# Second mixers of a hybrid model on one core: memory sums one step later, memory tiles one a beat, attention output turned behind two half products

## The chip, the core and the metric

The kernel runs on one core of one Trainium2 chip. The metric is the device time of the whole program in microseconds (us). The core has five engines that work through their own queues of instructions and wait for each other by semaphores: PE (TensorE, matrix products), ACT (ScalarE), DVE (VectorE), POOL (GpSimd) and SP (SyncE, which here issues the loads of the weights). PEld is PE's loading of the stationary operand, which overlaps its products.

## What is computed

A hybrid model of three layers on 512 tokens of width 1024, all in float32. The first layer and the final normalisation are not touched here. Two further layers follow, each: feed-forward, hybrid mixer, attention over a memory of 256 tokens, feed-forward.

```python
def second_block(x, mem, ...):
    for l in range(DEPTH_2):                      # 2
        y = swiglu_2(rms_norm(x, ffn1_pre_g[l]), ...)
        x = x + 0.5 * rms_norm(y, ffn1_post_g[l])
        y = hybrid_mixer(rms_norm(x, mix_pre_g[l]), w_in[l], ..., nsa_out_g[l], ret_gn_g[l], w_out[l])
        x = x + rms_norm(y, mix_post_g[l])
        y = memory_xattn(rms_norm(x, xa_pre_g[l]), rms_norm(mem, xa_mem_g[l]),
                         xa_wq[l], xa_wk[l], xa_wv[l], xa_wo[l])
        x = x + rms_norm(y, xa_post_g[l])
        y = swiglu_2(rms_norm(x, ffn2_pre_g[l]), ...)
        x = x + 0.5 * rms_norm(y, ffn2_post_g[l])
    return x

def hybrid_mixer(h, w_in, cmp_pe, cmp_w1, cmp_w2, nsa_out_g, ret_gn_g, w_out):
    parts = jnp.split(h @ w_in, IN_OFFSETS, axis=-1)
    ...
    o_nsa = rms_norm(nsa_mixer(...), nsa_out_g)    # attention: 8 heads, 3 branches
    o_ret = retention(...)                         # 4 heads, 4 chunks
    return jnp.concatenate([o_nsa, o_ret], axis=-1) @ w_out
```

`memory_xattn` needs the keys `rms_norm(mem) @ wk` and the values `rms_norm(mem) @ wv`. They don't depend on the tokens, and the kernel makes them inside the hybrid mixer.

## The kernel before

**Products.** Every float32 product is made of three: each operand is split into a high part (rounded to PE's fast format) and a low part (the rest), and `mm3` adds hi·hi, hi·lo and lo·hi in one PSUM bank (lines 251 to 253). Weights come in chunks of 1024 x 256, each as two halves of 128 x 1024. For each half SP loads `raw`, ACT copies it to `whi` (`weight_hi`, L234), and POOL subtracts `whi` from `raw` to give `wlo` (`weight_lo`, L246). There are four slots, so a chunk is split while the chunk two before it is in use: `weight_hi(k, ch.c + 2)` waits until that chunk has released its slot.

**The order.** Each engine's program is written out by hand as Python generators. A `yield` ends a *beat*. In `MixerTwo` the attention of 96 units (4 blocks of queries x 8 heads x 3 branches) sets the frame: in each step PE makes the scores of unit s (L933), turns the weights of unit s-1 (L944) and multiplies unit s-2 with the values (L957); DVE adds the bias and takes the maximum (L1000, L1004); ACT takes the exponent (L972) and copies the turned weights (L981). After each step come two beats of *filler*: products of the projections (`pe_filler`), 196 beats in all. Four streams run beside the filler: after every fourth beat one step of the memory's sums (from beat 8), of the retention (from beat 98), and of the norms of finished blocks of queries (from 60, 109, 157). All engines count the same beats; what one engine does in a beat and another needs in the same beat is thus close in time.

**The memory's root mean square.** `act_memory` squares one of eight tiles of the memory in each of its steps (L2219, 128 x 256, two buffers). `pe_memory` sums that square over the features in the same step with four small products (L342). In the step after the last square DVE takes the mean (L2336) and POOL the power -0.5 (L2373, `m_root`); one step further on PE spreads it over the rows (L2129) and ACT keeps the row (L2223). POOL's filler has a `weight_lo` of two halves every 16 beats, among them one at beat 48.

**The memory's tiles.** After the last gate chunk of the retention the filler makes the memory's high and low parts: ACT `xa_mhi` (L2205), DVE `xa_mlo` (L2321), two tiles in each of four beats in which PE has no filler. Then come four chunks of keys (`mkch`, all in banks 6 and 7) and four of values (`mvch`).

**The end of the mixer.** When the attention is done, the last block of queries is normalised: ACT square and sum (L2186), DVE mean (L2302), POOL power (L2357), DVE scaling (L2306). Then four times four blocks of it are turned by PE (`TurnTiles.pe`, L1506), and ACT and DVE make the high and low parts (L1514, L1521), which are the operands of w_out. w_out is done in four pairs of banks; the first two chunks, c0 and c1, are done by halves (`pe_out_half`): half 0 uses the retention's output, which is there earlier, half 1 the attention's.

## Time and profile before

| | us |
|---|---|
| median of 3 runs | 3539.95 |
| lowest and highest | 3537.64 and 3546.28 |
| the profiled execution, whole | 3543.9 |
| its span (first to last instruction) | 3542.6 |
| PE busy in the span | 3379.3 |
| ACT, DVE, POOL busy | 1225.6, 1373.4, 1275.5 |
| granted clock of PE, mean | 0.974 of full speed |

The profile lists one execution. Its own time is 3543.9 us, of which 1.3 us lie outside the span. Times in the trace are from the span's start. The first of the two mixers lies at about 1185 to 1635 us, the second at about 2550 to 3000 us; they do the same work in the same order. PE's clock has two levels in the records: 1.00 is 2.4 GHz, 0.50 is 1.2 GHz.

### The profile page before, as it was taken

Reading aid. Unit: us, or ns where it says so; the run is one execution under the profiler, and the core shown is the slowest. Engines: PE = TensorE matmul, PEld = TensorE weight load, DVE = VectorE, ACT = ScalarE, POOL = GpSimd, SP = SyncE. Lnnn points to the kernel's source line nnn. Section 1 sums busy time; section 2 is a strip of 40 time slices with the busy share of each in tenths; the row PEclk is TensorE's granted clock in tenths of the full one; section 3 lists DMA queues with packets and bytes.
Section 4 is the critical chain, followed back from the end, with each engine's and each line's share of the span. In section 5 each row is a group of like instructions: output and inputs, shape, how many; then the busy total and the mean of one; then the engine's idle time right before and its main releaser. Section 6 shows DMA issues by size and latency. Waiting matters only on the chain.

```text
span 3542.6 us, 42038 instructions
## 1 busy us (share of the span) xinstructions
PE 3379.3 (95%) x16296; PEld 2725.8 (77%) x16296; DVE 1373.4 (39%) x2531; ACT 1225.6 (35%) x2245; POOL 1275.5 (36%) x569
## 2 busy tenths in 40 slices
PE   5989999999999999999999999999989999999997
PEld 4876788887888767787678887888776877678886
DVE  4574443215330524654353304331334562534311
ACT  4444332223222433453332223222333444433221
POOL 3332244443444432132234443444351233224442
PEclk9999999999999989999999999999999999999999
DMA  3211122332333221121123222322231112112321
GB/s 126 79 55 53 51 92 96 97 99 79 98 101 98 89 90 44 42 72 66 58 80 99 98 98 75 107 95 94 79 125 48 37 61 83 60 60 95 99 98 66
DMA packets 79109, 287.05 MB, mean 81 GB/s; under 512 B 8896, under 2 KB 9152, under 8 KB 78400
## 3 DMA queue, kind: packets, MB, share of 16 engines
q1 hardware_dynamic: 77616, 278.42, 24.0%
q10 hardware_dynamic: 1296, 5.94, 0.4%
q8 instruction: 131, 2.15, 0.3%
q14 instruction: 66, 0.54, 0.0%
HBM read 282.23 MB, written 2.10 MB: 80 GB/s over the span
## 4 chain that ended last, share of the span: by engine, by line
PE 83%; DVE 7%; ACT 4%; POOL 3%; issue 3%; DMA 0%; ACTq 0%; POOLq 0%; DVEq 0%
PE bank L251 23%; PE bank L252 23%; PE bank L253 23%; PE bank L933 4%; PE bank L957 3%; POOL wlo L246 2%; PE bank L944 2%; ACT whi L234 1%; DVE hlo L620 1%; ACT hhi L668 1%; DVE x L615 1%; PE bank L2632 1%; DVE m_xbc L1542 1%; DVE m_V L2290 1%; PE bank L551 1%
## 5 line engine op out<-in xcount | busy, mean ns | idle before, releaser
L246 POOL TENSOR_TENSOR wlo<-raw,whi 128x1024 fp32r<-128x1024 f32 (+1 forms) x520 | 1230.6, 2367 | 2047.6 <-ACT whi L234 2012.7
L251 PE MATMUL bank<-hhi,whi 128*128 128x512 f32 x2416 | 971.1, 402 | 21.7 <-POOL wlo L246 10.2
L252 PE MATMUL bank<-hlo,whi 128*128 128x512 f32 x2456 | 963.8, 392 | 0.0
L253 PE MATMUL bank<-hhi,wlo 128*128 128x512 f32 x2416 | 949.2, 393 | 0.0
L234 ACT ACTIVATE whi<-raw 128x1024 fp32r<-128x1024 f32 (+1 forms) x536 | 533.7, 1034 | 377.0 <-PE bank L253 361.4
L251 PEld LDWEIGHTS bank<-hhi,whi 128*128 128x128 f32 x2416 | 458.6, 190 | 129.1 <-issue 33.0
L252 PEld LDWEIGHTS bank<-hlo,whi 128*128 128x128 f32 x2456 | 466.5, 190 | 91.6 <-issue 1.5
L253 PEld LDWEIGHTS bank<-hhi,wlo 128*128 128x128 f32 x2416 | 458.0, 190 | 98.0
L251 PE MATMUL bank<-ff_ahi,whi 128*128 128x512 f32 x880 | 342.8, 390 | 0.0
L253 PE MATMUL bank<-ff_ahi,wlo 128*128 128x512 f32 x880 | 342.4, 389 | 0.0
L252 PE MATMUL bank<-ff_alo,whi 128*128 128x512 f32 x840 | 326.8, 389 | 0.0
L493 DVE TENSOR_TENSOR tmp<-tmp,tmp 128x512 f32<-128x512 f32 x60 | 47.7, 795 | 577.4 <-ACT tmp L507 577.4
L972 ACT ACTIVATE att_s<-att_s,stat 128x128 f32<-128x128 f32 (+4 forms) x224 | 110.6, 494 | 426.9 <-DVE stat L1004 426.7
L846 ACT ACTIVATE ff_ahi<-tmp 128x512 fp32r<-128x512 f32 x110 | 69.6, 633 | 444.7 <-DVE tmp L869 444.7
L859 DVE TENSOR_TENSOR tmp<-bank,row 128x512 f32<-128x512 f32 x110 | 75.1, 690 | 365.0 <-PE bank L253 318.9
L253 PEld LDWEIGHTS bank<-ff_ahi,wlo 128*128 128x128 f32 x880 | 165.2, 188 | 34.6
L251 PEld LDWEIGHTS bank<-ff_ahi,whi 128*128 128x128 f32 x880 | 165.2, 188 | 34.0
L252 PEld LDWEIGHTS bank<-ff_alo,whi 128*128 128x128 f32 x840 | 157.7, 188 | 32.5
L1000 DVE SCALAR_TENSOR_TENSOR att_s<-consts,bank 128x32 f32<-128x32 f32 (+4 forms) x192 | 74.2, 386 | 273.6 <-PE bank L933 273.2
L840 ACT ACTIVATE tmp<-tmp 128x512 f32<-128x512 f32 x110 | 68.6, 630 | 308.4 <-DVE tmp L859 308.4
L867 DVE TENSOR_TENSOR tmp<-bank,row 128x512 f32<-128x512 f32 x110 | 75.9, 690 | 223.6 <-PE bank L253 223.6
L251 PE MATMUL bank<-whi,hhi 128*128 128x256 f32 x448 | 134.3, 300 | 0.0
(346 smaller groups left out, 4381.0 us busy)
## 6 DMA issues: line engine op xcount, KB each, us to landing
raw<-wstream SPq DMA_DIRECT2D x516, 512.0 KB, 3.7
raw<-wstream SPq DMA_DIRECT2D x20, 256.0 KB, 3.0
x<-xT ACTq DMA_DIRECT2D x4, 512.0 KB, 12.9
xa_v<-memT ACTq DMA_DIRECT2D x2, 1024.0 KB, 4.8
outT<-x SPq DMA_DIRECT2D x1, 2048.0 KB, 6.2
consts<-consts ACTq DMA_DIRECT2D x1, 1103.0 KB, 9.5
m_lw<-lru_w ACTq DMA_DIRECT2D x1, 544.0 KB, 3.4
par<-par SPq DMA_DIRECT2D x2, 248.0 KB, 13.9
```

Of the source, the lines that this page charges most:

```text
L234: a.activation(h.hi[:, 0:h.cols], h.raw[:, 0:h.cols], ACT.Copy).then_inc(h.hi_made.sem)
L246: g.tensor_tensor(h.lo[:, 0:h.cols], h.raw[:, 0:h.cols], h.hi[:, 0:h.cols].bitcast(F32), ALU.subtract).then_inc(h.lo_made.sem)
L251: t.matmul(out, l[0], r[0], start=start, stop=False)
L252: t.matmul(out, l[0], r[1], start=False, stop=False)
L253: return t.matmul(out, l[1], r[0], start=False, stop=stop)
L859: v.tensor_tensor(k.tmp[m][:, :], k.bank[gate.banks[m]][:, :], k.row[:, :], ALU.mult).then_inc(self.normed.sem)
L867: v.tensor_tensor(k.tmp[m][:, :], k.bank[up.banks[m]][:, :], k.row[:, :], ALU.mult).then_inc(self.up.sem)
L933: t.matmul(k.bank[b][:, 0:u["n"]], u["q"], u["k"], start=True, stop=True).then_inc(self.scores.sem)
L944: last = t.transpose(k.bank[b][0:rows, kb * P:(kb + 1) * P], s[:, kb * P:kb * P + rows], k.c("ident"))
L957: last = t.matmul(k.bank[b][:, at:at + DH], p[0:rows, kb * P:(kb + 1) * P], u["v"](kb), start=kb == 0, stop=kb == nb - 1, skip_group_check ...
L972: a.activation(s[:, 0:n], s[:, 0:n], ACT.Exp, bias=k.stat[:, 80 + step % 4:81 + step % 4], accum_out=self.sums(g)[0][:, step % group:step ...
L1000: v.scalar_tensor_tensor(s[:, 0:n], u["dist"], u["slope"], k.bank[b][:, 0:n], ALU.mult, ALU.add).then_inc(self.biased.sem)
```

## The change

It is made in `MixerTwo` alone (and one flag in a helper), so each part of it runs twice.

1. PE's sums of the squares run one memory step (four beats) behind ACT's squares. The mean on DVE, the power on POOL, the spreading on PE and the row on ACT come one to three steps later than before (DVE one, POOL and PE two, ACT three). DVE waits for the row just ahead of the first keys.
2. The memory's high and low parts are made one tile a beat in eight beats on ACT and DVE. PE starts the first key chunk after three empty beats instead of four, and takes it tile by tile (`pe_first_keys`: both banks for each tile) instead of bank by bank. DVE evicts both banks of that chunk in one beat.
3. At the end PE does half 0 of c0 and of c1 and then turns the attention's output, into four banks (0, 1, 4, 5) instead of two. The split of c1's weights moves on ACT and POOL from ahead of the last norm to behind it.

```diff
@@ MixerTwo.__init__
-        self.cat_nsa.takes(0, 1, 0, 1)
+        self.cat_nsa.takes(0, 1, 4, 5)
@@ MixerTwo.pe
         self.pe_out_half(c0, 0)
+        self.pe_out_half(c1, 0)
         run(self.cat_nsa.pe())
-        self.pe_out_half(c1, 0)
         self.pe_out_half(c0, 1)
         self.pe_out_half(c1, 1)
@@ pe_filler
-        yield from beats(4)
+        yield from beats(3)
         m = [self.mhi, self.mlo]
-        for c, ch in enumerate(self.mkch):
-            yield from pe_stationary(k, ch, lambda n: [a[:, n * MEM:(n + 1) * MEM] for a in m], KT, width=MEM,
-                                     ready=(lambda n: [self.m_lo[n]]) if c == 0 else None)
+        tile = lambda n: [a[:, n * MEM:(n + 1) * MEM] for a in m]
+        yield from self.pe_first_keys(self.mkch[0], tile)
+        for ch in self.mkch[1:]:
+            yield from pe_stationary(k, ch, tile, KT, width=MEM)
...
+    def pe_first_keys(self, ch, tile):
+        k, t = self.k, self.k.nc.tensor
+        for kk in range(KT):
+            pe_half_begin(k, ch, kk)
+            t.wait_ge(*self.m_lo[kk])
+            for m, b in enumerate(ch.banks):
+                if kk == 0 and ch.free[m] is not None:
+                    t.wait_ge(*ch.free[m])
+                last = mm3(k, k.bank[b][:, 0:MEM], ch.weights(kk, m * P, P), tile(kk), kk == 0, kk == KT - 1)
+                pe_step_end(ch, last, kk, kk == KT - 1, m == 1)
+            yield
@@ pe_memory
+        yield
         for n in range(KT):
             t.wait_ge(*self.m_sq[n])
...
-        yield
+        yield from beats(2)
         t.wait_ge(*self.m_root[0])
@@ act
         run(self.act_norm(3))
+        weight_hi(k, self.mvch[3].c + 2)
         weight_hi(k, self.out.chunks[0][4].c + 2, 0)
@@ act_filler
-            if n % 2:
-                yield
-        for c, ch in enumerate(self.mkch):
+            yield
+        yield from idle_act(k, self.mkch[0], 3)
+        for ch in self.mkch[1:]:
             yield from idle_act(k, ch, 8)
...
-            yield from keep_tokens_act(..., self.mv_kept, root=self.m_rs)
+            yield from keep_tokens_act(..., self.mv_kept, root=self.m_rs, then=c < 3)
@@ act_memory
-        yield
+        yield from beats(4)
         a.wait_ge(*self.m_rows[0])
@@ dve_filler
+        yield
         for n in range(KT):
...
-            if n % 2:
-                yield
+            yield
+        yield from beats(2)
+        v.wait_ge(*self.m_row[0])
         for c, ch in enumerate(self.mkch):
             for m, b in enumerate(ch.banks):
-                yield from beats(KT // 2)
+                yield from beats(KT // 2 if c > 0 else 0)
@@ dve_memory
-        yield from beats(KT)
+        yield from beats(KT + 1)
@@ pool
         run(self.pool_norm(3))
+        weight_lo(k, self.mvch[3].c + 2)
         self.out.pool()
@@ pool_filler
-        yield from beats(4)
-        for ch in self.mkch + self.mvch:
+        yield from beats(3)
+        for ch in self.mkch + self.mvch[0:3]:
             yield from idle_pool(k, ch, 8)
+        yield from beats(8)
@@ pool_memory
-        yield from beats(KT)
+        yield from beats(KT + 2)
         g.wait_ge(*self.m_mean[0])
```

**Place 1: POOL at beat 48 of the first of the two mixers.** `stat` is where the memory's mean and its root stand; `raw`, `whi`, `wlo` are the slots of the weights. The queue before:

```order
L246 TENSOR_TENSOR wlo2_61<-raw2_53,whi2_57 128x1024 [waits s_wlo,s_whi]
L246 TENSOR_TENSOR wlo3_62<-raw3_54,whi3_58 128x1024 [waits s_wlo,s_whi]
L2373 TENSOR_TENSOR stat_73<-stat_73,consts_71 128x2 [waits s_rstd_mean]
L246 TENSOR_TENSOR wlo0_59<-raw0_51,whi0_55 128x1024 [waits s_wlo,s_whi]
L246 TENSOR_TENSOR wlo1_60<-raw1_52,whi1_56 128x1024 [waits s_wlo,s_whi]
```

And now:

```order
L246 TENSOR_TENSOR wlo2_61<-raw2_53,whi2_57 128x1024 [waits s_wlo,s_whi]
L246 TENSOR_TENSOR wlo3_62<-raw3_54,whi3_58 128x1024 [waits s_wlo,s_whi]
L246 TENSOR_TENSOR wlo0_59<-raw0_51,whi0_55 128x1024 [waits s_wlo,s_whi]
L246 TENSOR_TENSOR wlo1_60<-raw1_52,whi1_56 128x1024 [waits s_wlo,s_whi]
L2393 TENSOR_TENSOR stat_73<-stat_73,consts_71 128x2 [waits s_rstd_mean]
```

The power for the memory's root has moved behind the two halves of a chunk's low part.

**Place 2: DVE where the memory's low parts begin, first mixer.** `m_gr` is the last gate of the retention, `att_s` and the maximum in `stat` belong to the next unit of the attention, `xa_mlo` is the memory's low part, `tmp_68` the retention's decayed scores. The queue before:

```order
L1084 SCALAR_TENSOR_TENSOR m_gr_121<-tmp_66,bank 128x256 [waits s_silu_tanh]
L2321 SCALAR_TENSOR_TENSOR xa_mlo_155<-xa_v_130,par_49,xa_mhi_154 128x256 [waits s_mem_hi] x4
L1000 SCALAR_TENSOR_TENSOR att_s_78_151<-consts,bank 128x384 [waits s_at_turned,s_at_scores]
L1004 TENSOR_REDUCE stat<-att_s_78_151 128x1 [waits s_at_exped,s_at_biased]
L2321 SCALAR_TENSOR_TENSOR xa_mlo_155<-xa_v_130,par_49,xa_mhi_154 128x256 [waits s_mem_hi] x2
```

And now:

```order
L1084 SCALAR_TENSOR_TENSOR m_gr_121<-tmp_66,bank 128x256 [waits s_silu_tanh]
L2340 SCALAR_TENSOR_TENSOR xa_mlo_155<-xa_v_130,par_49,xa_mhi_154 128x256 [waits s_mem_hi]
L1000 SCALAR_TENSOR_TENSOR att_s_78_151<-consts,bank 128x384 [waits s_at_turned,s_at_scores]
L1004 TENSOR_REDUCE stat<-att_s_78_151 128x1 [waits s_at_exped,s_at_biased]
L2340 SCALAR_TENSOR_TENSOR xa_mlo_155<-xa_v_130,par_49,xa_mhi_154 128x256 [waits s_mem_hi]
```

One low part instead of four stands ahead of the next unit's bias and maximum.

**Place 3: PE at the end of the mixer.** `m2_rethi` is the retention's output, `m2_otok` the attention's, `whi0` the weights of c0 and `whi2` those of c1 (half 0 of each), `whi1` half 1 of c0. The queue before:

```order
L253 MATMUL bank7<-m2_rethi_83_156,wlo0_59 128x512
L1506 MATMUL bank0<-consts_71,m2_otok_74_147 128x128 [waits s_at_biased,s_nsa_scaled]
L1506 MATMUL bank1<-consts_71,m2_otok_74_147 128x128 [waits s_at_biased,s_nsa_scaled]
...
L1506 MATMUL bank0<-consts_71,m2_otok_74_147 128x128 [waits s_cat_lo,s_nsa_scaled]
L1506 MATMUL bank1<-consts_71,m2_otok_74_147 128x128 [waits s_cat_lo,s_nsa_scaled]
...
L251 MATMUL bank2<-m2_rethi_83_156,whi2_57 128x512 [waits s_wlo,s_cat_lo,s_whi,s_at_kept]
```

And now, from the end of c1's half 0 on:

```order
L253 MATMUL bank3<-m2_rethi_83_156,wlo2_61 128x512
L1508 MATMUL bank0<-consts_71,m2_otok_74_147 128x128 [waits s_at_biased,s_nsa_scaled]
L1508 MATMUL bank1<-consts_71,m2_otok_74_147 128x128 [waits s_at_biased,s_nsa_scaled]
L1508 MATMUL bank4<-consts_71,m2_otok_74_147 128x128 [waits s_at_out,s_nsa_scaled]
L1508 MATMUL bank5<-consts_71,m2_otok_74_147 128x128 [waits s_cat_lo,s_nsa_scaled]
L251 MATMUL bank6<-m2_nsahi_85_158,whi1_56 128x512 [waits s_cat_lo,s_wlo,s_whi]
```

The turns have moved behind 24 more products (half 0 of c1), and the last two no longer wait for the low parts of the first two.

## Rows read from the trace of the kernel before

**Rows 1.** The page, part 1: busy time of each engine.

```profile
PE 3379.3 (95%) x16296; PEld 2725.8 (77%) x16296; DVE 1373.4 (39%) x2531; ACT 1225.6 (35%) x2245; POOL 1275.5 (36%) x569
```

**Rows 2.** Waits of PE, whole span: total us, times, longest us.

```profile
PE bank L944 <- ACT att_s L972: 21.5, 10, 6.9
...
PE bank L342 <- ACT tmp L2219: 12.0, 14, 2.4
...
PE bank L1506 <- DVE m_otok L2306: 8.3, 2, 4.2
```

**Rows 3.** Timeline of PE beside the sums: start, us, instruction, idle before.

```profile
1285.63 0.61 PE L342 MATMUL bank<-consts,tmp 128*128 128x1 f32 x4 [2.07 <-ACT tmp L2219]
...
1286.97 0.63 PE L933 MATMUL bank<-m_kc,m_q 64*128 64x32 f32 x2
...
1300.44 0.49 PE L933 MATMUL bank<-m_kc,m_q 64*128 64x32 f32 x2
...
1309.45 0.41 PE L933 MATMUL bank<-m_kc,m_q 64*128 64x32 f32 x2
```

**Rows 4.** Windows: stretch, its us, busy us (count) of PE, PEld, DVE, ACT, POOL, PEclk, DMA share, GB/s.

```profile
1287.00:1300.00 13.00, 13.00 (x38) 9.28 (x37) 3.83 (x11) 2.19 (x10) 2.25 (x1) 0.50 0.24 83
1318.00:1334.00 16.00, 16.00 (x44) 11.53 (x45) 3.53 (x14) 2.84 (x13) 2.05 (x2) 0.50 0.21 65
...
1345.00:1360.00 15.00, 15.00 (x74) 10.52 (x74) 7.72 (x23) 5.63 (x20) 4.50 (x2) 1.00 0.22 72
...
1471.00:1481.00 10.00, 5.06 (x22) 4.84 (x23) 7.01 (x14) 4.63 (x18) 2.01 (x1) 0.52 0.32 105
...
2656.00:2662.00 6.00, 6.00 (x17) 3.93 (x17) 1.09 (x4) 0.57 (x3) 2.73 (x2) 0.50 0.52 169
2683.00:2689.00 6.00, 6.00 (x17) 4.30 (x18) 0.57 (x2) 0.66 (x3) 3.38 (x2) 0.50 0.48 149
```

**Rows 5.** Timelines of POOL and PE around beats 40 to 52.

```profile
1332.24 0.70 POOL L2373 TENSOR_TENSOR stat<-stat,consts 128x2 f32<-128x2 f32 x1 [12.89 <-DVE stat L2336]
...
1344.72 4.92 POOL L246 TENSOR_TENSOR wlo<-raw,whi 128x1024 fp32r<-128x1024 f32 x2 [11.78 <-ACT whi L234]
...
1348.82 0.40 PE L253 MATMUL bank<-hhi,wlo 128*128 128x512 f32 x1
```

**Rows 6.** Timelines of POOL, DVE (first low part, then four merged) and PE at the memory's tiles.

```profile
1468.18 4.83 POOL L246 TENSOR_TENSOR wlo<-raw,whi 128x1024 fp32r<-128x1024 f32 x2 [19.64 <-ACT whi L234]
...
1469.48 1.33 DVE L2321 SCALAR_TENSOR_TENSOR xa_mlo<-xa_v,par,xa_mhi 128x256 fp32r<-128x256 f32 x1 [1.87 <-ACT xa_mhi L2205]
...
1469.48 4.61 DVE L2321 SCALAR_TENSOR_TENSOR xa_mlo<-xa_v,par,xa_mhi 128x256 fp32r<-128x256 f32 x4 [1.87 <-ACT xa_mhi L2205]
...
1475.94 0.90 PE L944 MATMUL bank<-consts,att_s 128*128 128x128 f32 x3 [6.91 <-ACT att_s L972]
...
1491.73 0.36 PE L251 MATMUL bank<-xa_mhi,whi 128*128 128x256 f32 x1
```

**Rows 7.** Timelines at the end of both mixers: PE, ACT, POOL, DVE.

```profile
1592.72 0.40 PE L251 MATMUL bank<-m_rethi,whi 128*128 128x512 f32 x1
...
1597.96 0.39 PE L253 MATMUL bank<-m_rethi,wlo 128*128 128x512 f32 x1
...
1614.47 0.39 PE L251 MATMUL bank<-m_nsahi,whi 128*128 128x512 f32 x1
...
1595.19 0.62 ACT L2186 ACTIVATE tmp<-m_otok 128x512 f32<-128x512 f32 x1
...
1599.31 0.55 POOL L2357 TENSOR_TENSOR stat<-stat,consts 128x1 f32<-128x1 f32 x1
...
1599.89 2.56 DVE L2306 TENSOR_SCALAR m_otok<-m_otok,stat 128x512 f32<-128x512 f32 x1 [3.80 <-POOL stat L2357]
...
2955.36 0.40 PE L251 MATMUL bank<-m_rethi,whi 128*128 128x512 f32 x1
...
2965.14 1.09 PE L1506 MATMUL bank<-consts,m_otok 128*128 128x128 f32 x8 [4.15 <-DVE m_otok L2306]
...
2976.54 0.39 PE L251 MATMUL bank<-m_nsahi,whi 128*128 128x512 f32 x1
```

More of the change, by code:

```diff
@@ L1108, in idle_act, with keep_tokens_act @@
     weight_hi(k, ch.c + 2)
-def keep_tokens_act(k, ch, dst, kept, n=256, root=None):
+def keep_tokens_act(k, ch, dst, kept, n=256, root=None, then=True):
     a = k.nc.scalar
@@ L1117, in keep_tokens_act @@
         a.activation(dst(tb), k.bank[b][:, 0:n], ACT.Copy, scale=1.0 if root is None else root[:, tb:tb + 1]).then_inc(kept.sem)
-    weight_hi(k, ch.c + 2)
+    if then:
+        weight_hi(k, ch.c + 2)
 def idle_dve(k, ch, steps):
```

5 lines of the change are left out of this document (1 added, 4 removed).

## The prediction

> **What bounds the kernel now.** PE does: it is busy 3379.3 us of a span of 3542.6, and DVE, POOL and ACT are busy for less than 40% of it [rows 1]. A change of order can only give back what PE waits, and what its products take too long for because its clock is at the lower level. So I read PE's waits first, then the granted clock around them, then the queues of the engines waited for. Three of PE's longest entries lie in the second mixers [rows 2]: the memory's sums wait 12.0 us in 14 places for ACT's squares; the attention waits once 6.91 us per mixer for an exponent (part of the 21.5); and the turns wait 4.2 us per mixer for the scaled output of the attention.
>
> The clock doubles the price. After a wait of 2.07 us at the sums the granted clock reads 0.50 (1.2 GHz instead of 2.4) for the 13 us that follow, and 0.50 again for at least 16 us at 1318 [rows 3, 4]. From 1286.97 to 1300.44 three steps of the attention take 13.47 us; the three steps from 1300.44 to 1309.45 take 9.01, with one sum more in them, which with its wait is some 0.9 us [rows 3]. So the work of 13.47 us takes 8.1 at full clock: a microsecond at 0.50 costs 0.4 us.
>
> **Part 1, the sums one step behind.** PE's sum n now needs a square that ACT made four beats earlier, two steps of the attention. The longest of those waits come where ACT has just split a chunk of weights ahead of the square; four beats cover that, since they take PE at least 5 us (two thirds of the 8.1 above) against the 2.1 or 2.5 us of lateness. ACT's square n needs PE's sum n-2, which PE now issues one memory step ahead of it, so no new wait arises on ACT. All 12.0 us of waiting go [rows 2]. With them the clock should stay up in this stretch: the four windows at 0.50 there are 13, 16, 6 and 6 us long [rows 4], 41 us, at 0.4 each 16.4 us. Together -28.4 us.
>
> The part adds a wait. POOL's power for the root now stands behind the low parts of beat 48 (place 1). These end at 1344.72 + 4.92 = 1349.64, the power takes 0.70 more, 1350.34 [rows 5]. PE asks for the root behind the product that starts at 1348.82 in the trace of before, so at about 1349.05. With 0.05 for the semaphore PE waits 1.35 us, in both mixers: +2.7 us. Queued behind it on PE is the next step of the attention, and DVE and ACT wait for that; no DMA is. No row has a wait of this size with PE loaded on both sides, so whether the clock falls behind it is open; I add 1.5 us for it in all, about a seventh of two stretches of 13 us at 0.4. The bounds of this term are 0 (if POOL starts its halves earlier) and 1.35 plus a stretch of 13 us at 0.4, so 6.6 us per mixer.
>
> **Part 2, the memory's tiles.** Here PE waits for an exponent, ACT for DVE's maximum, and DVE sits in its low parts: four of them take 4.61 us from 1469.48, the first alone 1.33, while POOL runs two halves of a low part from 1468.18 to 1473.01 [rows 6]. PE goes on at 1475.94, 1.85 us after the fourth low part ended at 1474.09. Now one low part stands ahead of the maximum (place 2). It ends at 1470.81, and with the same 1.85 us PE goes on at 1472.7, 3.3 us sooner. Before that, PE does the first tile of the keys in a part of this gap (it needs the first low part, 1470.81, and takes 0.7 us, so is done by 1471.6). From 1475.94 to the product at 1491.73 are 15.8 us, of which about 5 at the lower clock [rows 4, 6] cost 2.0; the same work at full clock takes 13.8. DVE's and ACT's single tiles put in two or three waits of PE below 0.8 us, and the later ones have eight beats; I take none net, as these tiles also leave the two slots they had. So PE arrives at 1486.5 instead of 1491.7, and with one beat of filler more done, 0.7 us: 5.9 us per mixer, 11.8 in both, if the clock stays up. It probably won't: PE still waits 2.2 us for the first tile and 0.8 for the exponent, and 2.07 us were enough at the sums [rows 3]. I put the lower clock at 60% in each mixer, about 9 us long, 3.5 us each: -4.2 of the gain. Part 2 gives -7.6 us, with bounds of 0 (each new wait as long as the old) and -11.8.
>
> DVE is held there because POOL is at work: its first low part takes 1.33 us and ends just behind POOL's first half [rows 6]. The Trainium skill (page "SBUF — State Buffer", section "Who interferes with whom") says why: a DVE instruction with two inputs in SBUF can't run beside a GpSimd instruction that reads SBUF, and the one that starts first keeps the other out. By that rule the first low part stays at 1.33 us after the change, since POOL's half starts ahead of it in the new order too; without the rule it could take a third of that (four of them take 4.61 us, of which the last three stand beside POOL in part only, so this is an estimate), and PE's wait would be some 0.9 us shorter in each mixer, the sum 1.8 us lower. The trace agrees with the rule.
>
> The first key chunk now frees both banks late and in one beat, and the next chunk needs bank 6 at once. Between the chunk's last product and that need PE has the retention's 16 products, and DVE two evictions of 128 x 256; these fit beside them, and I cost this at nothing. If they don't, PE waits for one of the two, which I put below 1 us per mixer.
>
> **Part 3, the turns.** Before, from the first product of c0 to the first that reads the attention's output: 1592.72 to 1614.47 is 21.75 us, and 2955.36 to 2976.54 is 21.18 [rows 7]. Now: half 0 of c0 takes 1597.96 + 0.23 - 1592.72 = 5.47 us, that of c1 the same; 16 turns take twice the 1.09 us of eight, 2.2; then 0.3 for low parts that come a little slower than PE uses them. Sum 13.4. That is 8.35 and 7.8 us less, 16.1 in both; the lower clock behind the wait is in it, 7 to 10 us long per mixer.
>
> This holds if c1's weights and the scaled output are in time. The square starts at about the same place as before (1595.19) or sooner, as ACT no longer splits c1 first; square, mean and power then take 0.75 + 0.2 + 0.6 us, since POOL isn't busy: the power stood at 1599.31 only because two halves of c1 ran ahead of it, and the scaling took 2.56 us beside a third [rows 7]. So the output is scaled by 1595 to 1598, and PE asks for it at 1603.7. c1's first half is split by ACT behind the square (1.0 us) and by POOL (2.4 us): about 1597.5, against PE's need at 1598.2. That margin is 0.7 us; where it fails, PE waits what is missing, at most 1 us. I take -15.9 us for the part.
>
> **Sum.** -28.4 + 2.7 + 1.5 - 7.6 - 15.9 = -47.7 us against the profiled execution, 3543.9: 3496. That execution is 4 us above the median of the three, and most of the difference between executions of one program is likely how long the clock is down; part of that is what the change removes. I predict 3493 us for the median.
>
> **Rivals.**
> 1. *The clock falls at each new wait.* The waits for the root and for the first tile are 1.35 and 2.2 us in each mixer. For it: 2.07 us sufficed [rows 3]. Against it: at the root PE is otherwise fully loaded. With 9 to 10 us at 0.50 behind each of the four, 15 us instead of the 5.7 in the sum: 3503, up to 3507. Chance 0.20.
> 2. *Nothing falls.* The clock stays up at all four: 5.7 us better than the sum, and 3486 with rounding for the small waits that I left in. Chance 0.10.
> 3. *The sums' waits only change their name.* If PE's waits at the sums only hide waits for ACT's exponents, which stand in the same queue behind the same splits of weights, they come back as waits for `att_s`, with the lower clock. Part 1 gives nothing: 3517. Against it: from 1345 to 1360, where ACT and POOL split weights and PE has no sum, PE is busy for 15.00 of 15.00 us at a clock of 1.00 [rows 4]. Chance 0.06.
> 4. *Slower.* Without the clock the parts save some 26 us of pure waiting and turning. What could eat that and the clock's share is PE held at 0.50 by the scattered small waits for single tiles over the whole stretch of keys and values, 100 us per mixer, instead of one window behind one long wait. It decides from about 130 us of 0.50 in the two mixers, where the trace of before has some 77 (the 41 of Part 1, and twice about 10 and 8 at the tiles and the turns); with 150 us the time is 3548. Chance 0.02.
>
> **Numbers.** The forecast has 0.60, its own range 3482 to 3501. A result within 0.3% (10.6 us, about what a measurement of this kernel can tell from no change) needs rival 4 in a weaker form: 0.02. Range 3480 to 3511, which takes in rivals 1 and most of 2 and leaves out 3 and 4. Faster by over 0.3%: 0.96 (the forecast and rivals 1 to 3), within: 0.02, slower: 0.02.
>
> **What would show it.** In the changed profile: no wait of PE on L342 above 0.3 us, and a clock of 1.00 from the first to the last sum; a wait on L2146 for POOL of 1.2 to 1.5 us in both mixers; at the first keys a wait for `xa_mlo` of about 2.2 us and one for `att_s` below 1, in place of 6.91; no wait on the turns (now L1508), which start 11 us behind c0's first product; 13 to 14 us from that to the first product with `m_nsahi`. I am wrong if waits for `att_s` in the stretch of the sums grow, if the turns still wait, or if a split of c1 comes after PE's need by more than 1 us.

## The result, and the profile after

The changed kernel takes 3492.8 us (median of 4 runs, 3492.6 to 3493.5) where the kernel before took 3539.3 in the same comparison: a ratio of 0.9864, with an interval from 0.9851 to 0.9877. The prediction was 3493. In a later comparison, below, the same program took 3500.6. The profiled execution of the changed kernel is 3493.5 us long, its span 3492.2, so 50.4 less than the span of before. The busy time of PE answers to [rows 1]: it fell by 31 us though PE does the same 16296 products.

```profile
PE 3348.5 (96%) x16296; PEld 2708.0 (78%) x16296; DVE 1385.1 (40%) x2531; ACT 1224.4 (35%) x2245; POOL 1275.6 (37%) x569
```

PE's waits over the whole span (total us, times, longest us) answer to [rows 2]. The entry for the squares and the one for the turns in the mixer are gone, the one for `att_s` has fallen from 21.5 to 14.9 only, and two entries are new:

```profile
PE bank L944 <- ACT att_s L972: 14.9, 14, 3.0
...
PE bank L251 <- DVE xa_mlo L2340: 4.8, 2, 2.4
...
PE bank L2146 <- POOL stat L2393: 2.3, 2, 1.1
```

The two programs give PE the same 96 score products per mixer in the same order, so their starts cut both traces into comparable stages. The windows of before, from the first to the 28th of them (the sums; both mixers), from the 66th to the 76th (the memory's tiles) and from there to the 91st (columns: stretch, its us, busy us and count of PE, PEld, DVE, ACT, POOL, granted clock, DMA share, GB/s):

```profile
1260.73:1349.85 89.12, 82.98 (x331) 57.06 (x330) 28.50 (x101) 27.94 (x98) 19.65 (x9) 0.83 0.16 53
...
1465.49:1510.85 45.36, 38.15 (x242) 31.04 (x241) 30.22 (x74) 21.02 (x66) 10.50 (x5) 0.89 0.15 47
1510.85:1566.29 55.44, 55.44 (x374) 44.48 (x373) 32.11 (x81) 28.80 (x74) 21.64 (x11) 1.00 0.23 77
2630.36:2713.02 82.66, 76.00 (x330) 51.81 (x330) 27.82 (x101) 27.88 (x98) 19.63 (x9) 0.92 0.17 57
```

The same stretches of the changed kernel:

```profile
1262.25:1331.97 69.72, 68.18 (x331) 48.42 (x330) 31.16 (x101) 27.38 (x97) 19.70 (x9) 1.00 0.22 72
...
1447.66:1488.71 41.05, 38.05 (x249) 31.10 (x248) 28.32 (x74) 22.68 (x68) 12.61 (x6) 0.96 0.16 52
1488.71:1549.57 60.86, 57.36 (x375) 45.91 (x374) 38.26 (x81) 27.25 (x72) 19.44 (x11) 0.97 0.22 70
2600.32:2670.04 69.72, 68.17 (x330) 48.42 (x330) 31.04 (x101) 27.32 (x97) 19.70 (x9) 1.00 0.22 72
```

The third row is the surprise: a stretch in which before had neither a wait nor a low clock is 5.42 us longer now. The rows of PE's timeline that mark the places (start, us, instruction, idle before and what ended it):

```profile
1330.63 0.71 PE L2146 MATMUL bank<-consts,stat 128*128 128x128 f32 x4 [1.12 <-POOL stat L2393]
...
1453.25 0.35 PE L251 MATMUL bank<-xa_mhi,whi 128*128 128x256 f32 x1 [2.38 <-DVE xa_mlo L2340]
...
1508.35 0.28 PE L944 MATMUL bank<-consts,att_s 128*32 128x128 f32 x1 [3.04 <-ACT att_s L972]
...
1575.27 0.40 PE L251 MATMUL bank<-m_rethi,whi 128*128 128x512 f32 x1
...
1586.18 1.91 PE L1508 MATMUL bank<-consts,m_otok 128*128 128x128 f32 x16
1588.44 0.47 PE L251 MATMUL bank<-m_nsahi,whi 128*128 128x512 f32 x1 [0.35 <-DVE m_nsalo L1523]
```

All stages together, in us of the two profiled executions:

| stage | first mixer | second mixer | both | predicted |
|---|---|---|---|---|
| sums and root (part 1) | 89.12 to 69.72 | 82.66 to 69.72 | -32.3 | -24.2 |
| memory's tiles (part 2) | 45.36 to 41.05 | 44.82 to 41.06 | -8.1 | -7.6, with the line after next |
| 76th to 91st score product | 55.44 to 60.86 | 55.44 to 60.86 | +10.8 | nothing |
| 91st to c0 (one beat less) | 26.43 to 25.70 | 26.44 to 25.71 | -1.5 | see above |
| c0 to the first `m_nsahi` (part 3) | 21.75 to 13.17 | 21.18 to 13.17 | -16.6 | -15.9 |
| all else | | | -2.8 | 0 |
| span | | | -50.4 | -47.7 |

"All else" is +1.5 ahead of the first attention, +0.1 between the 28th and the 66th product, -4.0 between the mixers and -0.4 behind the second, where the program is unchanged.

**Where the 10.8 us come from.** In the changed kernel DVE's centring of the retention's output (four pieces of 128 x 128 from SBUF to SBUF) takes 5.16 us, and the exponent of the next short unit stands behind it. Rows of DVE, POOL and ACT:

```profile
1502.04 5.16 DVE L2522 TENSOR_SCALAR m_qr<-m_qr,stat 128x128 f32<-128x128 f32 x4
1507.12 0.41 DVE L2348 TENSOR_TENSOR xa_k<-bank,tmp 128x256 f32<-128x256 f32 x1
1507.45 0.17 DVE L1000 SCALAR_TENSOR_TENSOR att_s<-consts,bank 128x32 f32<-128x32 f32 x1
...
1502.24 4.87 POOL L246 TENSOR_TENSOR wlo<-raw,whi 128x1024 fp32r<-128x1024 f32 x2 [9.36 <-ACT whi L234]
...
1501.12 2.00 ACT L234 ACTIVATE whi<-raw 128x1024 fp32r<-128x1024 f32 x2
...
1507.88 0.32 ACT L972 ACTIVATE att_s<-att_s,stat 128x32 f32<-128x32 f32 x1 [4.76 <-DVE stat L1004]
```

The centring ends at 1507.20, where POOL's two halves end (1507.11); ACT's split of the same chunk was over at 1503.12, so it isn't what holds DVE. Before, the same centring took 0.87 us, and POOL's low parts began 2.3 us after it had ended:

```profile
1524.18 0.87 DVE L2503 TENSOR_SCALAR m_qr<-m_qr,stat 128x128 f32<-128x128 f32 x4
...
1527.33 4.89 POOL L246 TENSOR_TENSOR wlo<-raw,whi 128x1024 fp32r<-128x1024 f32 x2 [9.34 <-ACT whi L234]
```

The filler has one beat less since the change, and the retention's steps stand at fixed beats. So the splits of weights behind the memory's tiles have moved one beat against the retention: the one that stands at the end of the third key chunk (it splits the weights two chunks on, those of the first value chunk) from beat 156 to 155, next to the retention's step of beat 154. My theory after these traces: part 1 gave more than predicted, part 2's gain was eaten by this collision, and the two errors cancelled. The rival: the working of the prediction was right, and what looks like a shift between parts is that the clock happened to fall otherwise in these two executions.

### The profile page after: what moved, and what is told of

It reads as the page before. It is cut to its first block, busy times and chain, and to the rows that moved or that the text cites. A ratio compares the mean times of both kernels' runs of the same rounds, so it can differ in the third digit from the quotient of the medians.

```text
span 3492.2 us, 42040 instructions
## 1 busy us (share of the span) xinstructions
PE 3348.5 (96%) x16296; PEld 2708.0 (78%) x16296; DVE 1385.1 (40%) x2531; ACT 1224.4 (35%) x2245; POOL 1275.6 (37%) x569
## 4 chain that ended last, share of the span: by engine, by line
PE 82%; DVE 8%; ACT 3%; POOL 3%; issue 3%; DMA 0%; ACTq 0%; POOLq 0%; DVEq 0%
PE bank L251 24%; PE bank L253 23%; PE bank L252 23%; PE bank L933 4%; PE bank L957 3%; POOL wlo L246 2%; PE bank L944 2%; DVE hlo L620 1%; ACT hhi L668 1%; DVE x L615 1%; ACT whi L234 1%; PE bank L2651 1%; DVE m_xbc L1544 1%; DVE m_V L2308 1%; PE bank L551 1%
## 5 line engine op out<-in xcount | busy, mean ns | idle before, releaser
L493 DVE TENSOR_TENSOR tmp<-tmp,tmp 128x512 f32<-128x512 f32 x60 | 47.7, 795 | 562.5 <-ACT tmp L507 562.5
```

## Experiments

"Split" is below the pair of ACT's `whi` and POOL's `wlo` of one chunk. Where a time stands it is a median of at least 4 runs; the others ran once, and their trace is read and not their time. Those single times are 3496.0 to 3501.1 us for the changed kernel with an edit, and 3548.2 for y_before155, with 3546.2 for before beside it.

### Each part alone

p1_sums: only the part of the diff on `pe_memory`, `act_memory`, `dve_memory`, `pool_memory`, with DVE's wait for the row ahead of the first keys (in `dve_filler`):

```diff
@@ pe_memory
+        yield
         for n in range(KT):
...
-        yield
+        yield from beats(2)
@@ act_memory
-        yield
+        yield from beats(4)
@@ dve_filler, ahead of the first keys
+        v.wait_ge(*self.m_row[0])
@@ dve_memory
-        yield from beats(KT)
+        yield from beats(KT + 1)
...
@@ pool_memory
-        yield from beats(KT)
+        yield from beats(KT + 2)
```

> Part 1 of the change alone on the kernel before. Theory A (the two traces read stage by stage: the prediction sized this part too small, because a microsecond at the lower clock costs PE the full 0.5 us and not 0.4, and there were 44 of them beside the sums): about 32 us less than before, 3507 to 3508, with no wait of PE for the squares, a wait of 1.1 us for the root in each mixer, and a clock of 1.00 from 1280 to 1350. Rival B (the working of the prediction holds, and the rest of what the whole change gained here belongs to the other parts): 24 us less, 3515 to 3516.

3513.8 us against 3541.7 of before: ratio 0.9922 (0.9905 to 0.9938), 27.8 us less. Window of the sums in the first mixer, and the new wait:

```profile
1262.73:1332.44 69.71, 68.17 (x330) 48.41 (x329) 31.15 (x101) 27.39 (x97) 19.69 (x9) 1.00 0.22 72
```

```profile
1331.11 0.71 PE L2130 MATMUL bank<-consts,stat 128*128 128x128 f32 x4 [1.12 <-POOL stat L2373]
```

The stage is as long as with the whole change (69.71 us, and 69.72 in the second mixer), so what the table shows there comes from this part alone. The median fell by less than the table's 32.3 us, and that difference lies in the execution of before: its two stages (89.12 and 82.66 us) are long ones. The six of other traces with the old sums have a mean of 83.3, and from that to 69.72 it is 27.2 us for both mixers, close to the 27.8 of the medians. The span of this trace, 3512.1, is 30.5 below that of before, 1.8 less than the stages give, because other stretches were longer, such as the one behind the second mixer (568 us for 566), where the program is the same; and the profiled execution of before lay 2.2 above the median it is compared with here. Theory A is right on what went and what came in this stage, but its time was too low by 6, because its 32 us come from that long execution. By the medians rival B (3515 to 3516) was nearer: 27.8 us lies midway between its 24 and the 32.

p2_tiles: only the parts of the diff on the memory's tiles, the first key chunk and the missing beat.

```diff
@@ pe_filler
-        yield from beats(4)
+        yield from beats(3)
...
+        yield from self.pe_first_keys(self.mkch[0], tile)
... (act_filler and dve_filler as in the whole change, without the wait for the row)
@@ pool_filler
-        yield from beats(4)
+        yield from beats(3)
```

> Part 2 alone on the kernel before. Theory A (its gain at the first keys, about 4 us a mixer, is eaten by a new wait of 3.0 us and the lower clock behind it, because the split of a key chunk on POOL now stands at beat 155 instead of 156 and runs beside the retention's centring on DVE): no change, 3538 to 3543, with a wait of PE on att_s of about 3 us at the second half of the keys in both mixers, and the centring (DVE, m_qr in four pieces) at about 5.2 us instead of 0.87. Rival B (the working of the prediction): 7.6 us less, 3532, and the new wait is made by parts 1 or 3 and isn't in this trace.

3541.0 against 3541.7: ratio 1.000 (0.999 to 1.001). Rows of DVE and PE:

```profile
1519.97 5.16 DVE L2518 TENSOR_SCALAR m_qr<-m_qr,stat 128x128 f32<-128x128 f32 x4
```

```profile
1526.28 0.28 PE L944 MATMUL bank<-consts,att_s 128*32 128x128 f32 x1 [3.04 <-ACT att_s L972]
```

The wait and the slow centring are there without parts 1 and 3. Theory A holds: part 2 by itself brings nothing that the medians show.

p3_turns: only the order of the turns, their banks and the split of c1.

```diff
...
         self.pe_out_half(c0, 0)
+        self.pe_out_half(c1, 0)
         run(self.cat_nsa.pe())
-        self.pe_out_half(c1, 0)
...
@@ act, and the like in pool
         run(self.act_norm(3))
+        weight_hi(k, self.mvch[3].c + 2)
```

> Part 3 alone on the kernel before. Theory A: its two gains are in its own stretch, from the first product of c0 to the first with m_nsahi 13.2 us instead of 21.75 and 21.18, so 16 to 17 us less, 3523. Rival B (part of it is the neighbourhood: without part 1 and 2 the last norm comes later, and c1's split behind it is late for PE): 13 us less or fewer, a wait of PE for wlo in c1.

3524.3 against 3541.7: ratio 0.9953 (0.9936 to 0.9969), 17.3 less. From c0 to the first `m_nsahi` it takes 13.17 us in both mixers, as with the whole change; the turns follow without a wait:

```profile
1598.41 1.91 PE L1508 MATMUL bank<-consts,m_otok 128*128 128x128 f32 x16
1600.67 0.47 PE L251 MATMUL bank<-m_nsahi,whi 128*128 128x512 f32 x1 [0.35 <-DVE m_nsalo L1523]
```

The three together are 27.8 + 0.7 + 17.3 = 45.8 us, where the whole change gave 46.5 in its own comparison and 39.3 in the later one (after_again, below). So by the medians the parts add up only as far as such comparisons agree, to some 7 us. The traces say more: each part's stage is as long alone as in the whole change, to 0.1 us, except that of the tiles, where the clock varies.

### The collision

x_keys156: the changed kernel, with the one split back at beat 156.

```diff
@@ act_filler
-        for ch in self.mkch[1:]:
-            yield from idle_act(k, ch, 8)
+        for ch, n in zip(self.mkch[1:], (8, 9, 7)):
+            yield from idle_act(k, ch, n)
@@ pool_filler
-        for ch in self.mkch + self.mvch[0:3]:
-            yield from idle_pool(k, ch, 8)
+        for ch, n in zip(self.mkch + self.mvch[0:3], (8, 8, 9, 7, 8, 8, 8)):
+            yield from idle_pool(k, ch, n)
```

> The changed kernel with one edit: ACT and POOL split the weights of the key chunk of beat 155 one beat later, at 156, as before the change. Theory A (collision of DVE's centring with POOL's low part): the centring is back at about 0.87 us for four pieces, PE's wait of 3.04 us in each mixer is gone and so are the 3.4 us at the lower clock behind it (1.7 us), so 9.5 us less than the changed kernel, 3483 to 3484. Rival B (the centring is slow for another reason, its place behind the exponent of the longest unit or its own semaphores): DVE keeps its 5.2 us and the time stays 3493. Rival C: the collision only moves to another pair of instructions: wait gone here, one of 1 to 3 us elsewhere between beats 150 and 165, 3486 to 3493.

3489.3 us (3486.6 to 3496.1). The window from the 76th to the 91st score product, then DVE and POOL:

```profile
1494.16:1549.94 55.78, 55.52 (x374) 44.42 (x373) 34.90 (x81) 27.13 (x72) 19.50 (x11) 1.00 0.24 76
```

```profile
1507.49 0.87 DVE L2522 TENSOR_SCALAR m_qr<-m_qr,stat 128x128 f32<-128x128 f32 x4
...
1510.96 4.91 POOL L246 TENSOR_TENSOR wlo<-raw,whi 128x1024 fp32r<-128x1024 f32 x2 [12.63 <-ACT whi L234]
```

By the trace theory A is right: 0.87 us again, no wait, the clock at 1.00, and the stage 5.08 us shorter in each mixer. (It is still 0.34 above the 55.44 of before.) By the time the 3483 to 3484 expected were missed, and this run alone doesn't show the 10 us: it is 3.5 below the changed kernel's 3492.8 of the first comparison and 11.3 below the 3500.6 of the later one, and the changed kernel did not run beside it. x_best below ran beside it, but has this edit together with two others.

y_before155: the kernel before, with that split moved from beat 156 to 155 on ACT and POOL. No other operation of POOL stands between the two beats, so only ACT's queue has another order than before; the order on PE, DVE and POOL stays.

```diff
@@ act_filler
-        for c, ch in enumerate(self.mkch):
-            yield from idle_act(k, ch, 8)
+        for ch, n in zip(self.mkch, (8, 8, 7, 9)):
+            yield from idle_act(k, ch, n)
@@ pool_filler
-        for ch in self.mkch + self.mvch:
-            yield from idle_pool(k, ch, 8)
+        for ch, n in zip(self.mkch + self.mvch, (8, 8, 7, 9, 8, 8, 8, 8)):
+            yield from idle_pool(k, ch, n)
```

> The kernel before, with nothing but ACT's split of one key chunk moved from beat 156 to 155; the order on PE, DVE and POOL is unchanged. Theory A (the collision needs nothing else of the change): DVE's centring of m_qr (four pieces) takes about 5.2 us instead of 0.87, PE waits about 3 us for att_s behind it in both mixers, and the stretch from the 76th to the 91st score product is 60.5 to 61 us instead of 55.44. Rival B (the changed kernel's first key chunk, one beat earlier on PE and evicted later, is part of it): no such wait, 55.4 us.

Rows of DVE, POOL and PE:

```profile
1518.63 5.16 DVE L2503 TENSOR_SCALAR m_qr<-m_qr,stat 128x128 f32<-128x128 f32 x4
```

```profile
1518.84 4.87 POOL L246 TENSOR_TENSOR wlo<-raw,whi 128x1024 fp32r<-128x1024 f32 x2 [6.39 <-ACT whi L234]
```

```profile
1524.61 0.40 PE L944 MATMUL bank<-consts,att_s 128*32 128x128 f32 x1 [2.71 <-ACT att_s L972]
```

The stage is 60.91 and 63.22 us long instead of 55.44; the second is 2.2 above the 61 expected, with the clock at a mean of 0.92 where the first mixer has 0.94. One beat of one split is enough, on a kernel that has nothing else of the change. Rival B falls but for 0.3 us: the wait is 2.71 and not 3.04, because in the changed kernel the eviction of a key chunk (`xa_k`, 0.41 us) also stands ahead of the next unit's bias on DVE, where in the kernel before it stands behind.

### The wait ahead of the first tile

x_tile_pool: POOL's half of the split of beat 128 also waits for the first low part.

```diff
@@ pool_filler
+        k.nc.gpsimd.wait_ge(*self.m_lo[0])
         weight_lo(k, self.grch[1].c + 2)
```

> The changed kernel with one wait added: POOL begins the low parts of the chunk of beat 128 only when DVE has made the memory's first low part. Nothing else moves; ACT still splits the chunk ahead of the memory's high parts. Theory A (a low part of DVE, two operands in SBUF, is held while POOL subtracts): the first xa_mlo takes 0.45 to 0.5 us instead of 1.33 and PE's wait ahead of the first tile falls from 2.38 to about 1.5 us in both mixers; the second low part, which then meets POOL, gets longer. Rival B (the first low part is slow because ACT writes the next high part beside it): 1.33 and 2.38 us stay.

In the changed kernel the first low part, beside POOL, reads:

```profile
1451.66 1.33 DVE L2340 SCALAR_TENSOR_TENSOR xa_mlo<-xa_v,par,xa_mhi 128x256 fp32r<-128x256 f32 x1 [1.87 <-ACT xa_mhi L2223]
```

Here, with POOL held back, and PE behind it:

```profile
1451.21 0.48 DVE L2340 SCALAR_TENSOR_TENSOR xa_mlo<-xa_v,par,xa_mhi 128x256 fp32r<-128x256 f32 x1 [1.87 <-ACT xa_mhi L2223]
...
1452.66 1.76 DVE L2340 SCALAR_TENSOR_TENSOR xa_mlo<-xa_v,par,xa_mhi 128x256 fp32r<-128x256 f32 x1
```

```profile
1451.95 0.55 PE L251 MATMUL bank<-xa_mhi,whi 128*128 128x256 f32 x1 [1.53 <-DVE xa_mlo L2340]
```

Theory A to the number: 0.48 instead of 1.33, the wait 1.53 (1.56 in the second mixer) instead of 2.38, and the second low part, which now meets POOL, takes 1.76. But the stage gained nothing by it: it is 41.18 and 43.38 us long, with the clock at a mean of 0.92 and 0.88 instead of 0.96. ACT's split of that chunk stands ahead of the memory's first high part in ACT's queue; that the remaining 1.5 us are its doing is shown by the next run, where it moves as well and they go.

x_tile130: both halves of that split two beats later.

```diff
@@ act_filler, among the memory's high parts
+            if n == 2:
+                weight_hi(k, self.grch[1].c + 2)
             yield
@@ pool_filler
+        yield from idle_pool(k, self.grch[1], 18)
+        yield from beats(1)
```

> The changed kernel, with ACT's split of the chunk of beat 128 moved two beats later, behind the memory's third high part (POOL's follows it). Theory A (the wait ahead of the first tile is that split, 2.0 us on ACT, and the 0.85 us that POOL adds to DVE): no wait ahead of the first tile in either mixer, the clock stays at 1.00, about 2.4 + 1.7 us less per mixer, the stretch from the 66th to the 76th score product 37 us instead of 41.05. Rival B: the fourth high part and the exponents now stand behind the 2 us, and POOL's halves beside the low parts 2 to 4: a wait of 1 to 3 us for xa_mlo or att_s two to four beats later, and the stretch stays at 39 to 41 us.

The first tile is in time in both mixers, but two waits have come in its place, and DVE's two low parts beside POOL take 3.07 us:

```profile
1454.96 0.28 PE L944 MATMUL bank<-consts,att_s 128*32 128x128 f32 x1 [0.96 <-ACT att_s L972]
1457.37 0.39 PE L251 MATMUL bank<-xa_mhi,whi 128*128 128x256 f32 x1 [1.15 <-DVE xa_mlo L2343]
```

```profile
1454.64 3.07 DVE L2343 SCALAR_TENSOR_TENSOR xa_mlo<-xa_v,par,xa_mhi 128x256 fp32r<-128x256 f32 x2 [2.37 <-ACT xa_mhi L2224]
```

The stage takes 41.10 and 43.79 us, no less than with the wait, where theory A had 37. Rival B is right here: among the tiles the split only makes other waits.

### The wait for the root

x_root44: POOL's power one memory step earlier, ahead of the chunk of beat 48.

```diff
@@ pool_memory
-        yield from beats(KT + 2)
+        yield from beats(KT + 1)
```

> The changed kernel with POOL's power for the memory's root one memory step earlier, ahead of the chunk of beat 48 in its queue. Theory A: PE's wait of 1.12 us on the root is gone in both mixers and nothing takes its place; the stretch of the sums (first to 28th score product) 68.6 us instead of 69.72. Rival B: POOL now waits for DVE's mean and its halves come later, so that PE waits for wlo of that chunk: over 0.3 us on L251 between 1320 and 1350.

No wait on L2146, and none of POOL's low parts late. The window of the sums:

```profile
1263.89:1332.21 68.32, 67.90 (x330) 48.49 (x329) 31.14 (x101) 27.39 (x97) 19.74 (x9) 1.00 0.21 70
```

1.40 us less than in the changed kernel, as theory A had it. The wait was made by the order of POOL's queue alone.

### The changed kernel again, and all three waits away

after_again is the changed kernel without an edit.

> The changed kernel once more, on the same chip as the next one, so that the two can be compared. Both theories: 3493; how far it lies from that says how much of the difference between kernels is the lower clock outside the mixers, which fell for 110 us in all in its first trace and for 141 in the trace with the key chunk's split at beat 156.

3500.6 us (3498.8 to 3502.9) against 3539.9 of before: ratio 0.9886 (0.9869 to 0.9902). So the same program is 7.8 us slower here than in the first comparison, while the kernel before is not. Its runs have a mean granted clock of 0.981 to 0.983, those of the first comparison 0.984 and 0.985. Why is not shown. The later comparison ran on another chip than the experiments above, and which one the first ran on isn't known. The two traces differ by 5.3 us, of which 2.1 lie ahead of the first mixer's attention and 3.6 in its stage of the tiles:

```profile
1449.69:1494.31 44.62, 41.94 (x249) 34.31 (x248) 28.60 (x74) 22.68 (x68) 12.60 (x6) 0.85 0.15 48
```

It has the same waits as the 41.05 us above, but the clock stands at 0.85 instead of 0.96 of its level. The second mixer of the same execution took 41.06 again.

x_best: the changed kernel with the power at its earlier place, the split of 155 at 156, and the split of beat 128 behind all tiles.

```diff
@@ act_filler, among the memory's high parts
+            if n == 7:
+                weight_hi(k, self.grch[1].c + 2)
             yield
@@ pool_filler
-        yield from beats(3)
-        for ch in self.mkch + self.mvch[0:3]:
-            yield from idle_pool(k, ch, 8)
+        yield from idle_pool(k, self.grch[1], 23)
+        for ch, n in zip(self.mkch + self.mvch[0:3], (4, 8, 9, 7, 8, 8, 8)):
+            yield from idle_pool(k, ch, n)
@@ pool_memory
-        yield from beats(KT + 2)
+        yield from beats(KT + 1)
```

> The changed kernel with three edits: the power for the root ahead of the chunk of beat 48 on POOL; the split of the chunk of beat 128 behind all eight tiles of the memory on ACT (beat 135) and POOL; the split of the chunk of beat 155 at 156. Theory A (each of the three new waits is made by what stands ahead in another engine's queue or runs beside it, and goes with it): per mixer 1.4 us less at the sums, about 4.4 from the 66th to the 76th score product (36.7 instead of 41.05, with the clock at 1.00) and 5.1 from the 76th to the 91st, so 21 to 22 us less than the changed kernel, 3471, if the clock elsewhere is the same. Rival B (the chunk split at 135 comes too late for PE at beat 139, or POOL's halves now hold DVE's gates of the retention and the exponent behind them): a wait of 1 to 4 us on L251 for wlo or on L944 near beat 139, and 3480 or more. Rival C (the lower clock follows any load of this kind, so it appears elsewhere when these waits are gone): waits gone, but the time falls by less than 14 us.

3478.3 us (3472.3 to 3479.5): ratio to before 0.9817 (0.9803 to 0.9832), and 22.3 below the changed kernel beside it, where 21 to 22 were expected (the time of 3471 was missed with the 3493 it was worked out from). The three stages give 1.4 + 3.1 + 5.1 us per mixer against the first trace of the changed kernel, and 3.6 more against the 44.62 above: 22.7. The two traced executions themselves differ by 20.4 only, so the closeness to 22.3 is in part chance. The windows:

```profile
1261.95:1330.28 68.33, 67.91 (x330) 48.50 (x330) 31.17 (x101) 27.40 (x97) 19.73 (x9) 1.00 0.21 70
1445.97:1483.95 37.98, 36.62 (x249) 29.57 (x248) 28.30 (x74) 22.83 (x68) 12.63 (x6) 1.00 0.18 56
1483.95:1539.74 55.79, 55.53 (x374) 44.42 (x374) 34.93 (x81) 27.15 (x72) 19.52 (x11) 1.00 0.23 76
```

The clock reads 1.00 in all three. The middle one is 1.3 us above the 36.7 expected. Rows of PE and DVE tell why:

```profile
1464.90 0.39 PE L251 MATMUL bank<-xa_mhi,whi 128*128 128x256 f32 x1 [0.87 <-DVE xa_k L2351]
```

```profile
1459.09 1.67 DVE L2343 SCALAR_TENSOR_TENSOR xa_mlo<-xa_v,par,xa_mhi 128x256 fp32r<-128x256 f32 x1
...
1460.99 2.02 DVE L1012 TENSOR_SCALAR stat<-stat 128x3 f32<-128x3 f32 x1
```

The moved low parts now hold DVE by 1.2 us at the last tile and by 1.9 at a scalar operation of three columns; the evictions of the first key chunk come late behind them, and PE waits 0.87 for the bank. Rival B named the right cause, POOL's halves holding DVE, but waits of 1 to 4 us in other places; the split stands behind all eight tiles on ACT and still meets the last of them on DVE.

### Which half of part 3 does the work

x_turns_first: the turns back between half 0 of c0 and half 0 of c1 on PE; the split of c1 stays behind the norm.

```diff
         self.pe_out_half(c0, 0)
+        run(self.cat_nsa.pe())
         self.pe_out_half(c1, 0)
-        run(self.cat_nsa.pe())
```

> The changed kernel with the turns of the attention's output back between half 0 of c0 and half 0 of c1 on PE; the four banks and the later split of c1's weights stay. Theory A (the gain of part 3 comes from taking c1's split away from ahead of the norm, so that the output is scaled 2.6 us behind c0's first product, before half 0 of c0 ends at 5.5): no wait of PE on the turns here either, and from c0's first product to the first with m_nsahi 12.8 to 13.2 us, as in the changed kernel (13.17). Rival B (the order on PE is what hides the norm): a wait of over 1 us on L1508 and 15 us or more.

Rows of PE and DVE (c0 starts at 1574.37):

```profile
1579.85 1.91 PE L1508 MATMUL bank<-consts,m_otok 128*128 128x128 f32 x16
...
1587.05 0.39 PE L251 MATMUL bank<-m_nsahi,whi 128*128 128x512 f32 x1
```

```profile
1576.51 0.49 DVE L2324 TENSOR_SCALAR m_otok<-m_otok,stat 128x512 f32<-128x512 f32 x1 [0.67 <-POOL stat L2376]
```

No wait on the turns, and 12.68 us from c0 to the first `m_nsahi`: half a microsecond better than the changed order, because the low parts are made while PE does c1.

x_split_first: the other way round. The split of c1 is back ahead of the norm, the turns stay behind both half products.

```diff
         run(self.act_norm(3))
-        weight_hi(k, self.mvch[3].c + 2)
```

> The changed kernel with the split of c1's weights on ACT and POOL back where it stood, ahead of the last norm; the order on PE (turns behind half 0 of c1) and the four banks stay. With the run before it, this takes the two halves of part 3 apart. Theory A (either half alone hides the norm): the output is scaled as late as before, 9.7 us behind c0's first product, but PE asks for it only at 10.9, so no wait over 0.3 us on the turns and 13.2 to 13.6 us from c0's first product to the first with m_nsahi. Rival B (the late split carries the gain, the order on PE carries none): a wait of over 1 us on the turns, 14.5 us or more.

Rows of DVE and PE (c0 starts at 1580.49):

```profile
1587.69 2.60 DVE L2323 TENSOR_SCALAR m_otok<-m_otok,stat 128x512 f32<-128x512 f32 x1 [3.83 <-POOL stat L2374]
```

```profile
1591.41 1.91 PE L1508 MATMUL bank<-consts,m_otok 128*128 128x128 f32 x16
1593.66 0.47 PE L251 MATMUL bank<-m_nsahi,whi 128*128 128x512 f32 x1 [0.35 <-DVE m_nsalo L1523]
```

The output is scaled 9.8 us behind c0, as late as before, and PE asks for it at 10.9: no wait, 13.17 us. In both runs theory A holds. With the four banks, which stay in both runs, either half of part 3 brings its whole gain; with both, one is to spare. What the banks bring by themselves was not tested.

## Why the prediction was right, point by point

The time was right to a microsecond, the sum behind it wasn't. Against the traces two terms missed by 8 and 11 us with opposite signs. The sum of the working was 3496, and the 3493 came from taking 3 us off because the profiled execution of before was a slow one.

- **The sums: mechanism right, the clock's term mis-sized.** The 12.0 us of waits went, as did the lower clock: 1.00 from the first to the last sum. The term was -28.4 with +4.2 for the new wait, together -24.2; the stages of the two profiled executions show -32.3. Idle time of PE in the stage fell from 6.14 and 6.66 us to 1.54 and 1.55, which is 9.7. The other 22.6 are PE's busy time, where I had 16.4: 41 us at 0.4. The 0.4 came from comparing three steps of 13.47 us with three later ones of 9.01, from which I took off the sum and its wait. With the clock up the very same three steps take 7.54, not 8.1, so a microsecond there cost 0.44. Cut into threes of steps, 20.2 of the 22.6 us lie where the clock of before reads below 0.99, some 44 us at half speed, 0.46 each; the last 2.4 lie where it reads 0.99 or 1.00, and what they are is not shown. Of the miss of 8.1 us, 6.2 are this term, 1.5 the clock behind the root, which did not fall, and 0.4 the waits. Across medians the part is worth 27.8 only. In the three other traces that have the old sums (p2_tiles, p3_turns, y_before155) the stage takes 82.2 to 85.3 us in the six mixers, 83.3 in the mean, which is 13.6 above 69.72 and 27.2 for two; the 89.12 of the profiled execution of before is the longest of all. So 5.2 of the 32.3 us, and of the miss, are the execution that the prediction was worked out from; against an ordinary one the term was 3 us too small.
- **The wait for the root: right.** Predicted 1.35 us in each mixer, measured 1.12 and 1.13. In this trace it cost no clock; I had 1.5 us for that.
- **The memory's tiles: right at the place.** Predicted waits of 2.2 us for `xa_mlo` and under 0.8 for the exponent; measured 2.38 and 0.32, and 2.41 and 0.28. The clock fell in both mixers, but for less: 0.96 over 41.05 us is 3.3 us at half speed instead of the 9 of the prediction. That is luck of this execution: in four of seven traces with this wait the first mixer's stage took 44.1 to 44.6 us. With the beat saved at the end the part gave -9.5 there against the -7.6 predicted.
- **What the prediction left out: +10.8 us.** The step that failed is the term for what stands behind the tiles: the prediction takes the small waits as "none net", lets PE arrive 5.9 us earlier and costs nothing on the way to the end of the keys. It looked at what the diff moves and not at what stands still while all else moves: the retention's steps keep their beats, the splits behind the tiles come one beat earlier. The trace of before had the price in it: POOL's low parts hold DVE [rows 6], and the centring stood 2.3 us ahead of one. The cited section of the Trainium skill (page "SBUF — State Buffer", "Who interferes with whom") names `tensor_scalar` beside the instructions with two inputs: it can enter a mode with two ports, in which it too takes the pair shared with GpSimd. This case's trace agrees: 5.16 us beside POOL, 0.87 alone. I had used only its sentence on two inputs.
- **The turns: right, -16.6 against -15.9.** No wait on L1508, the turns 10.9 us behind c0's first product, 13.17 us to the first `m_nsahi`, where 13.4 were worked out; the wait for its low part 0.35 instead of 0.3. The split of c1 came in time. That either half suffices was in the numbers of the prediction (before, the output was scaled 9.7 us behind c0's first product; PE was to ask for it after 11.0), but not seen there.
- **The rivals.** Neither "the clock falls at each new wait" nor "nothing falls" happened: it fell at the tiles and at the unforeseen wait, and not at the root. The sums' waits did not come back under another name, and nothing held PE over the whole stretch of keys. Rival 4's numbers don't follow from the price of 0.4 used elsewhere: the 26 us saved would be used up at 142 us of lower clock (77 + 65), not 130, and 150 us would give 3543, not 3548. The forecast and its range don't use these numbers.

The rest, -2.8 us in the spans, lies where the program is the same. How far one program's time goes apart is shown by the 7.8 us between two medians of the changed kernel. An agreement to 0.2 us is chance, and the later median would have missed by 7.6; the size of the terms is what can be judged.

## What to carry to other kernels

When a change takes one beat out of a stream, list everything that does not move with it, and look at each pair that now meets: here one beat cost as much as the part it belonged to had gained. Where DVE works from SBUF beside POOL's large subtractions, keep a gap between them, and try such a subtraction behind the whole group of small operations that PE waits for, not ahead of it or between them (38.0 us for the stage here instead of 41 or more). A wait at the end of a phase can be taken away from either side, by a later question or an earlier answer; find the one that is enough before doing both.

## What the runs showed of the hardware

- A DVE operation with one data input in SBUF was held by POOL like one with two. The centring of four 128 x 128 pieces takes 5.16 us beside two of POOL's halves and 0.87 alone, and one of 128 x 3 took 2.02 us where it takes 0.16 alone. Both end within 0.1 us of POOL's second half. DVE's bias on the scores (one input from PSUM) and its reductions keep their time beside POOL: 0.54 and 0.55 us for 128 x 384 at 1452.9 in the changed kernel, 0.55 and 0.55 without POOL.
- The same wait doesn't always cost the same clock. Behind the wait of 2.4 us at the first tile the stage was 41.05 or 41.06 us long in three of the four mixers in the changed kernel's two traces, and 44.62 in the fourth, with the clock at a mean of 0.85 instead of 0.96. In all seven traces with that wait the stage took 41.05 to 44.62 us in the first mixer (43.3 in the mean) and 41.03 to 41.94 in the second.
- Behind the 1.1 us for the root, with PE loaded on both sides, the clock stayed at 1.00 in most traces, but in x_tile_pool it fell in both mixers, where the program is the same up to there: the stage of the sums took 70.71 and 70.81 us instead of 69.72, and from 1329 to 1331 the clock reads 0.50. In these runs a short wait was a risk to the clock, not a fixed price.
